# Token mixing in one streaming layer: the gates' weight block holds its own low part, and the output norm's sum is taken in two fp32r parts

## The reference, cut to what matters

```
h = rms_norm(x, norm1)                  # positions x 1024
p = h @ w_in                            # 3080 columns: u 512 | v 512 | q 512 | k 512 | v_B 512 | z 512 | beta 4 | a 4
beta = sigmoid(b_raw)
g = -exp(a_log) * softplus(a_raw + dt_bias)
q, k, v = silu(causal_conv(q, k, v));  q = l2norm(q) * 128**-0.5;  k = l2norm(k)
o, S = gated delta rule over q, k, v, g, beta   # 4 heads of 128 x 128 state
o = rms_norm(o, gdn_norm) * silu(z)             # norm over the 128 values of a head
x = x + concat([y_a, o]) @ w_o
```

## Time and profile before

| what | value |
|---|---|
| median of 3 runs | 2660.67 us |
| the profiled execution's own time | 2660.4 us |
| its span, first to last instruction | 2658.7 us |
| TensorE (PE) busy | 2588.7 us, 97% |
| VectorE (DVE) busy | 1830.7 us, 69% |
| ScalarE (ACT) busy | 1221.3 us, 46% |
| GpSimd (POOL) busy | 28.0 us, 1% |
| DMA queue of the kernel | 322.63 MB, 39.2% of 16 engines |

### The profile page before, as it was taken

The page is one execution under the profiler, slowest core; times in us unless marked ns, Lnnn a source line. Parts: engine busy times, 40 slices in busy tenths (PEclk is TensorE's granted clock), DMA queues, the critical chain, the costliest instruction groups (busy, mean ns, idle before and its releaser), DMA issues.

```text
span 2658.7 us, 47276 instructions
## 1 busy us (share of the span) xinstructions
PE 2588.7 (97%) x18469; PEld 2276.9 (86%) x18469; DVE 1830.7 (69%) x3335; ACT 1221.3 (46%) x2267; POOL 28.0 (1%) x72
## 2 busy tenths in 40 slices
PE   8999999999999999789999999999999998999998
PEld 7878777777777777589999998999999998999997
DVE  4666776677667657587677677766666667777766
ACT  3435555655655656444243436424343345433444
POOL 1000000000000000000000000000000000000000
PEclk9999999999999999999999999999999999999999
DMA  9356444454544646543232325413121251322321
GB/s 312 102 155 176 143 128 139 123 167 114 167 124 131 207 159 211 201 138 113 72 113 78 100 79 166 155 48 96 48 88 56 72 186 52 94 66 80 96 88 56
DMA packets 372255, 325.67 MB, mean 122 GB/s; under 512 B 13985, under 2 KB 314130, under 8 KB 369986
## 3 DMA queue, kind: packets, MB, share of 16 engines
q1 hardware_dynamic: 371650, 322.63, 39.2%
q0 software_dynamic: 384, 0.02, 0.0%
HBM read 261.09 MB, written 61.51 MB: 121 GB/s over the span
## 4 chain that ended last, share of the span: by engine, by line
PE 53%; DVE 3%; ACT 1%; issue 0%; DMA 0%; DVEq 0%; ACTq 0%
PE down_ps L3363 8%; PE down_ps L3364 8%; PE down_ps L3365 8%; PE gate_ps L3368 3%; PE gate_ps L3370 3%; PE gate_ps L3369 3%; PE up_ps L3368 3%; PE up_ps L3369 3%; PE up_ps L3370 3%; PE down_ps L3370 1%; PE down_ps L3369 1%; PE down_ps L3368 1%; PE gate_ps L3363 1%; PE gate_ps L3365 1%; PE gate_ps L3364 1%; PE up_ps L3365 1%
## 5 line engine op out<-in xcount | busy, mean ns | idle before, releaser
L1679 PE MATMUL pr_p<-hT_hi_p,w_hi_p 128*128 128x512 f32 x992 | 419.5, 423 | 2.1 <-ACT w_in_sb L748 1.1
L1681 PE MATMUL pr_p<-hT_hi_p,w_lo_p 128*128 128x512 f32 x992 | 388.7, 392 | 0.0
L1680 PE MATMUL pr_p<-hT_lo_p,w_hi_p 128*128 128x512 f32 x992 | 388.5, 392 | 0.0
L3111 DVE TENSOR_TENSOR middle<-down_ps,middle 128x512 f32<-128x512 f32 x374 | 257.3, 690 | 162.2 <-PE down_ps L3365 160.3
L3363 PE MATMUL down_ps<-wd_hi,act_hi 128*128 128x512 f32 x748 | 291.5, 390 | 5.6 <-DVE act_lo L3099 5.6
L3364 PE MATMUL down_ps<-wd_lo,act_hi 128*128 128x512 f32 x748 | 291.5, 390 | 0.0
L3365 PE MATMUL down_ps<-wd_hi,act_lo 128*128 128x512 f32 x748 | 291.4, 390 | 0.0
L2947 DVE TENSOR_TENSOR w_ring<-w_in_sb,w_ring 128x512 fp32r<-128x512 f32 x264 | 181.5, 687 | 73.2 <-ACT w_ring L2659 71.3
L1679 PEld LDWEIGHTS pr_p<-hT_hi_p,w_hi_p 128*128 128x128 f32 x992 | 186.9, 188 | 42.1 <-issue 7.2
L1681 PEld LDWEIGHTS pr_p<-hT_hi_p,w_lo_p 128*128 128x128 f32 x992 | 186.6, 188 | 41.5
L1100 DVE TENSOR_TENSOR w_lo_p<-w_in_sb,w_hi_p 128x1024 fp32r<-128x1024 f32 x124 | 150.7, 1216 | 103.2 <-ACT w_hi_p L728 103.0
(11 more groups left out here) (485 smaller groups left out, 5570.3 us busy)
## 6 DMA issues: line engine op xcount, KB each, us to landing
w_in_sb<-in_w_in SPq DMA_DIRECT2D x100, 512.0 KB, 4.4
raws<-in_w_down SPq DMA_DIRECT2D x66, 512.0 KB, 3.7
w_in_sb<-in_w_gate SPq DMA_DIRECT2D x128, 256.0 KB, 3.1
w_in_sb<-in_w_up SPq DMA_DIRECT2D x128, 256.0 KB, 3.4
stream_tiles<-w_in_sb SPq DMA_DIRECT2D x96, 256.0 KB, 2.5
w_in_sb<-stream_tiles SPq DMA_DIRECT2D x16, 1280.0 KB, 7.6
w_in_sb<-mixed_tiles SPq DMA_DIRECT2D x29, 512.0 KB, 4.7
w_in_sb<-in_w_in SPq DMA_DIRECT2D x5, 2048.0 KB, 15.1
```

Source lines behind the costliest of these rows:

```text
L1679: pe.matmul(out, w_h, x_h, start=start, stop=False)
L1680: pe.matmul(out, w_h, x_l, start=False, stop=False)
L1681: return pe.matmul(out, w_l, x_h, start=False, stop=stop)
L3111: dve.tensor_tensor(part, half_ps[i % (2 * NH)], part, ALU.add).then_inc(half_added, 1)
```

## The change

The gates' item loses its low-part matmuls. VectorE writes the low part of the 8 gate columns into 8 of the unused columns (112 to 119) of the item's high block, so that two matmuls (by the high and by the low rows) give, in rows 112 to 119 of the result, the product of the low weights, and in rows 120 to 127 that of the high ones. `turn_gates` then doesn't transpose: for each of the four tiles it multiplies the 128 x 128 block of rows by 8 columns of the identity, twice into the same 8 columns of PSUM, which turns and adds the two parts.

The output norm's sum over partitions is made as the other norm's is: VectorE copies the sum of squares to fp32r (`sq_a_hi`) and makes the remainder (`sq_a_lo`), and two fp32r matmuls replace the fp32 one. The two buffers are shared with the other norm, so ScalarE waits for the earlier output norm before it writes `sq_a_hi`, and VectorE for the matmuls of this tile's other norm.

```
 # ScalarE, gmlp_squares
                 past(act, s["ssa_pe"], t)
+                past(act, s["sso_pe"], t)
                 act.activation(sq_a[:], ya[:], ACT.Square).then_inc(s["sq_a_ready"], 1)
 # VectorE, split_weights
                     dve.wait_ge(s["w_hi_ready"], n + 1)
+                    if kind(n) == "ba":
+                        dve.tensor_tensor(w_hi[:, n % RING_W, :, P - 4 * H_B:P - 2 * H_B], wraw[:, n % 2, :, P - 2 * H_B:],
+                                          w_hi[:, n % RING_W, :, P - 2 * H_B:].bitcast(F32), ALU.subtract)\
+                           .then_inc(s["w_lo_ready"], 1)
+                        return
 # VectorE, sum_squares
                 dve.tensor_tensor(sq_p, sq_p, sq_q[:], ALU.add).then_inc(s["sq_sum_ready"], 1)
+                past(dve, s["ssa_pe"], t + 1)
+                dve.wait_ge(s["sq_sum_ready"], 3 * t + 1)
+                dve.tensor_copy(sq_a_hi[:], sq_p).then_inc(s["sq_sum_ready"], 1)
+                dve.wait_ge(s["sq_sum_ready"], 3 * t + 2)
+                dve.tensor_tensor(sq_a_lo[:], sq_p, sq_a_hi[:].bitcast(F32), ALU.subtract).then_inc(s["sq_sum_ready"], 1)
 # TensorE, quarter
+                    if kind(n) == "ba":
+                        pe.matmul(pr[n % 2][:], w_hi[:, w, k], hT_hi[:, k], start=k == 0, stop=False)
+                        last = pe.matmul(pr[n % 2][:], w_hi[:, w, k], hT_lo[:, k], start=False, stop=k == KC - 1)
+                        continue
                     last = three(pr[n % 2][:], w_hi[:, w, k], w_lo[:, w, k], hT_hi[:, k], hT_lo[:, k],
 # TensorE, turn_gates
-                    last = pe.transpose(gs[:, i * P:(i + 1) * P], ba[:, i * P:(i + 1) * P], sh["ident"][:])
+                    to, rows = gs[:, (i + 1) * P - 2 * H_B:(i + 1) * P], ba[:, i * P:(i + 1) * P]
+                    pe.matmul(to, rows, sh["ident"][:, P - 4 * H_B:P - 2 * H_B], start=True, stop=False)
+                    last = pe.matmul(to, rows, sh["ident"][:, P - 2 * H_B:], start=False, stop=True)
 # TensorE, output_norm
-                pe.wait_ge(s["sq_sum_ready"], t + 1)
-                pe.matmul(gb[4][:], sh["ones"][:], flat(sq_p), start=True, stop=True).then_inc(s["sso_pe"], 1)
+                pe.wait_ge(s["sq_sum_ready"], 3 * t + 3)
+                over_partitions(gb[4][:], "ones_r", sq_a_hi[:], sq_a_lo[:]).then_inc(s["sso_pe"], 1)
```

## The result

The changed kernel takes 2673.32 us, the median of 8 runs (2670.38 to 2675.98); the kernel before took 2661.6 in 8 runs beside it. The ratio is 1.0038, 95% interval 1.0028 to 1.0047: slower by 10 us by the ratio and by 11.7 us by the medians, above the predicted range. The profiled execution took 2673.4 us, its span is 2671.6.

What follows compares the result with a forecast made beforehand. PE, busy for 97% of the span, was taken to bound the kernel. Items 0, turns +5.1, norms −4.0 and +2.9 made +4.0; with +1.7 for the clock, 2660.4 became about 2666 us, range 2657.5 to 2671.5.

Steps and rivals of the forecast that it cites:

- the items' 7.3 us: Gates' items, four with 8 of 24 matmuls fewer: 7.3 us less PE work, of which 0 was taken to arrive.
- the row of the same form: Profile row of eight fp32 matmuls, two passes each, 1.71 us: 0.107 a pass, used to price the gates' turn.
- the rival in which the passes go without a reload: Gates' turn: passes cost no block reload, so −5.1 us, about 2661 with the clock drop, 2659 without; chance 0.06.
- the six slots named: Output norm in slots 3, 7, 11, 13, 14 and 15: hardly any slack, stalls of over 1 us there alone.
- the sum's −4.0 + 2.9: Output norm: −4.0 us from ten slots with slack, +2.9 from the six slots with hardly any.
- The part of the sum without the clock, +4.0: Whole change at unchanged clock: items 0, turns +5.1, norms −4.0 and +2.9, giving +4.0, 2664.4 us.
- the term for the lower clock: Behind four waits lengthened to about 2 or 3 us: about one drop to half clock, +1.7 us.
- six waits late in the kernel: Waits of like size late in the kernel, two counted with a clock drop; the basis for the drop rate.
- "paid in full": Gates' turn in slots −3, 1, 5 and 9: 1.27 us more each, followed at once by more PE work.
- The rival on the slower side: Clock falls after three or four lengthened waits, item 2 and `level_lx` in slots 0, 4, 8: 2669.5 to 2671.2; chance 0.20.
- The prediction's own sign of being wrong: Mixing phase ending earlier than 1118 us or more than 8 us later, or the unchanged phase behind it moving.

Runs made afterwards that it cites:

- with macro tile 0 as before: Changed kernel, but macro tile 0 keeps its gates' item of 24 matmuls and its turn as four transposes: 2670.11 us, ratio 1.0025 to the kernel before.
- run 512: Not a follow-up run: "run" is a verb here, and 512 is the column count of matmuls that PE had executed up to the wait.
- The variant with the norm in the slack slots: Kernel before with the two-part output norm in ten slots only; slots 3, 7, 11, 13, 14, 15 keep the fp32 matmul: 2656.69 us, ratio 0.9972.

## Why the prediction was wrong

**Right, by its own steps.** Nothing of the items' 7.3 us arrived: the waits at item 2 and at `level_lx` in slots 0, 4 and 8 became 2.87, 1.88, 1.81 and 1.79 (2.9 and "2 to 3" were forecast). The turn costs 1.70 us for 16 passes, as the row of the same form gave it, and 0.81 for 8; the rival in which the passes go without a reload has fallen. The Trainium skill ("TensorE: Matmul & The Clock Gate", section "LDWEIGHTS (loading the stationary operand)") gives a weight load P / 1.2 ns for P columns, which makes an estimated 107 ns for 128; the trace's 0.11 us from pass to pass agrees. The gap of some 25 ns that the Trainium skill ("TensorE: Matmul & The Clock Gate", section "Back-to-back issue gap") gives a small matmul by itself shows in this stream at most once a turn: the first two passes take 126.50 − 126.36 = 0.14 us, the next pairs 0.22. The norm gave 0.41 in ten slots (0.37 to 0.39 in the changed kernel), VectorE's cast took 0.43 us, as here in slot 3,

```profile
467.15 0.69 DVE L1588 TENSOR_TENSOR w_in_sb<-w_in_sb,sq_q_p 128x512 f32<-128x512 f32 x1
467.94 0.43 DVE L1591 CAST sq_a_hi_p<-w_in_sb 128x512 fp32r<-128x512 f32 x1
468.40 0.69 DVE L1593 TENSOR_TENSOR sq_a_lo_p<-w_in_sb,sq_a_hi_p 128x512 fp32r<-128x512 f32 x1
```

and the stalls came in the six slots named and in no other. Each stall moved TensorE by some 0.86 in slots 3, 7, 11 and 13 (0.73 forecast), by 0.5 in slot 14 and by 1.26 in slot 15; the next `level_lx` took back 0.67 behind slot 3, all of it behind slot 7 and 0.35 behind slot 11. With the norm alone the balance is −1.1, the sum's −4.0 + 2.9. The part of the sum without the clock, +4.0, stands: turns 5.3, norms −1.1 (−0.8 in the changed kernel), items 0.

**The step that failed** is the term for the lower clock, "four thirds is about one drop, +1.7". The runs show about 7.2 us in the changed kernel's profile (1.4, 3.3, 1.0 and, not tied to the change, 1.5). The term was wrong in two ways:

- Its rate was one in three, from six waits late in the kernel. That count itself was low: the feed-forward of that trace has six waits of 1.8 to 3.9 us, and the clock is low behind three, of 1.81, 1.92 and 3.91 us (the last is in the line below). Behind the lengthened waits of the mixing it fell in 5 of 5 cases at item 2 and 9 of 15 at `level_lx`. Its price was too high: +1.4 behind item 2, and at `level_lx` 1.4 to 1.5, of which a later wait in the slot takes back 0.5 to 0.57, so that 0.9 to 1.0 is left.
- It looked for low clock behind waits alone. Slot −3 had 6.83 us at 0.50 in the kernel before, ahead of any change: the turn, then 64 passes by 32 columns. The prediction priced the turn there as "paid in full" at 1.27 us. With it the stretch lasted 10.2 to 17.1 us, and each microsecond more at 0.50 cost half of one: +3.3 in the changed kernel, +5.0 with the turn alone. The short item alone lengthened it too, to 10.2 us (+1.6), so the changed kernel's 3.3 can't be divided between the two; with macro tile 0 as before it is gone. PE never waits there; it has small matmuls.

```profile
2237.00:2243.70 6.70, 5.53 (x21) 5.56 (x22) 6.70 (x9) 5.61 (x10) 0.00 (x0) 0.50 0.27 81
```

The rival on the slower side had the right mechanism, 5.1 to 6.8 us of low clock, but all of it at the four waits. With two of these places, slot −3 and slot 14 the result came out above its 2671.2. The prediction's own sign of being wrong was there: the mixing phase ends more than 8 us later. A smaller part is the base: the profile at 2660.4 was a low draw of a kernel whose medians were 2661.6 to 2664.2 in four sets of runs.

**Open.** The variant with the norm in the slack slots gained 7.5 us by medians where its timeline gains 4.8; its mean granted clock over the runs is 0.9920 against 0.9913 beside it, some 4 us less at the lower level, about 2 of the 3 us left (an estimate; the difference is about twice its own uncertainty). Why the clock was higher wasn't tried. Nor was it settled why the stretch of slot −3 is 10 us in one execution and 14 in the next of the same kernel, or how a short item some 50 us ahead lengthens it.

## What to carry to other kernels

Work taken from a busy engine ahead of a wait that another engine ends is no gain, and on TensorE it can cost: here the longer idling was followed by the lower clock, and eight matmuls fewer in each of four items made the kernel slower. Before pricing an edit at its own duration, list the stretches where the granted clock is low already, and see whether the edit puts small matmuls beside one or more idling ahead of other work. A change that gains in ten slots and stalls in six can be made in the ten: this alone beat both kernels.

## What was not expected of the hardware

Full items directly behind the wait of 2.87 us ran with the clock at 0.50 for some 3 us, though PE had run 512-column matmuls up to the wait. And a busy PE lost the clock too: with the turn alone it was busy in slot −3 for all of the 16.80 us at 0.50. Up to 139.09 us that was fp32 passes by 32 columns, with the turn's passes by 8 just ahead at the full clock; behind it full items ran at 0.50 for another 5 us.
